# Attention in a fused three-layer kernel: the eight query products, one run of 24 matmuls each, divided into blocks between the scores and the weights

## The reference, cut to what matters

```python
def nsa_mixer(h, w_q, w_o, k_cmp, v_cmp, k_sel, v_sel, k_win, v_win):
    proj = h @ w_q
    q = proj[..., :NSA_HEADS * NSA_HEAD_DIM].reshape(bsz, s_len, NSA_KV_HEADS, NSA_GROUP, NSA_HEAD_DIM)
    q_rot = partial_rope(q, jnp.arange(s_len))
    ...
        s = jnp.einsum("bqhgd,bchd->bhgqc", qc, k_cmp) * scale
        p_cmp = masked_softmax(s, (cmp_end[None, :] <= t[:, None])[None, None, None], axis=-1)
        ...
        o = g[..., 0:1] * o_cmp + g[..., 1:2] * o_sel + g[..., 2:3] * o_win
```

## Time and profile before

| what | value |
|---|---|
| median of three runs | 2632.68 us |
| span of the profiled execution | 2629.4 us |
| TensorE, ScalarE, VectorE, GpSimd busy | 96%, 41%, 46%, 37% |
| mean granted TensorE clock | 0.990 |
| attention steps on TensorE | from 929.7 to about 1161 us |

### The profile page before, as it was taken

One profiled execution on the slowest core, in us unless ns is written; L12 is line 12 of the kernel. 1 busy time (PEld: TensorE's weight loads), 2 busy tenths in 40 slices (PEclk: granted clock), 3 DMA queues, 4 the chain that ended last, 5 costly groups with the idle time before them and its releaser, 6 DMA issues.

```text
span 2629.4 us, 36734 instructions
## 1 busy us (share of the span) xinstructions
PE 2511.7 (96%) x13336; PEld 2048.5 (78%) x13336; DVE 1204.0 (46%) x2013; ACT 1067.6 (41%) x1678; POOL 976.4 (37%) x431
## 2 busy tenths in 40 slices
PE   4999989999999989999999999999899999999998
PEld 2877768888888756669888888788668888988887
DVE  6777776656545657645111127653122112631112
ACT  3466644322224346655222236734442323542232
POOL 1433334555554210024444443302114455353453
PEclk9999999999999999999999999999999999999999
DMA  6533344577653210012333232201113333232331
GB/s 255 182 106 120 105 126 131 190 243 237 216 177 130 93 36 19 19 43 66 100 97 105 89 103 69 76 9 56 42 32 101 105 107 113 64 111 87 98 105 56
DMA packets 75762, 277.33 MB, mean 105 GB/s; under 512 B 8528, under 2 KB 10960, under 8 KB 74224
## 3 DMA queue, kind: packets, MB, share of 16 engines
q1 hardware_dynamic: 56672, 201.66, 24.4%
q10 hardware_dynamic: 18960, 73.87, 8.1%
HBM read 272.54 MB, written 2.16 MB: 104 GB/s over the span
## 4 chain that ended last, share of the span: by engine, by line
PE 84%; DVE 7%; ACT 3%; issue 2%; DMA 2%; ACTq 1%; SPq 0%; DVEq 0%
PE G L293 30%; PE STAT_G L293 30%; PE B L306 2%; PE B L587 2%; PE B L293 2%; PE B L2398 1%; DMA const<-in_const 1%; PE B L1342 1%; PE STAT_G L306 1%; PE G L306 1%; PE NRM L1379 1%; ACTq L1108 1%; PE G L587 1%; PE STAT_G L587 1%; PE B L1671 1%
## 5 line engine op out<-in xcount | busy, mean ns | idle before, releaser
L278 POOL TENSOR_TENSOR w_lo<-raw,w_hi 128x1024 fp32r<-128x1024 f32 x375 | 937.5, 2512 | 1601.8 <-ACT w_hi L270 1585.6
L270 ACT ACTIVATE w_hi<-raw 128x1024 fp32r<-128x1024 f32 x375 | 386.4, 1051 | 308.7 <-PE STAT_G L293 127.3
L293 PE MATMUL G<-h_hi,w_hi 128*128 128x512 f32 x888 | 352.0, 396 | 0.1
L293 PE MATMUL STAT_G<-h_hi,w_hi 128*128 128x512 f32 x872 | 344.9, 396 | 3.0 <-ACT mod_w L1227 1.6
L293 PE MATMUL G<-h_lo,w_hi 128*128 128x512 f32 x888 | 346.7, 390 | 0.0
L293 PE MATMUL G<-h_hi,w_lo 128*128 128x512 f32 x888 | 346.7, 390 | 0.0
L293 PE MATMUL STAT_G<-h_lo,w_hi 128*128 128x512 f32 x872 | 339.9, 390 | 0.0
L293 PE MATMUL STAT_G<-h_hi,w_lo 128*128 128x512 f32 x872 | 339.8, 390 | 0.0
L347 DVE SCALAR_TENSOR_TENSOR mod_w<-mod_w,const 128x1024 f32<-128x1024 f32 x96 | 178.9, 1880 | 51.8 <-DMA mod_w<-in_modw 51.4
L293 PEld LDWEIGHTS G<-h_hi,w_hi 128*128 128x128 f32 x888 | 167.4, 189 | 38.7 <-issue 4.2
L293 PEld LDWEIGHTS G<-h_lo,w_hi 128*128 128x128 f32 x888 | 167.5, 189 | 35.3 <-issue 1.4
(11 more groups left out here) (562 smaller groups left out, 4341.4 us busy)
## 6 DMA issues: line engine op xcount, KB each, us to landing
raw<-in_units SPq DMA_DIRECT2D x375, 512.0 KB, 3.6
mod_w<-in_modw ACTq DMA_DIRECT2D x96, 512.0 KB, 4.9
mod_first<-in_modw ACTq DMA_DIRECT2D x8, 1024.0 KB, 21.1
acsb<-acs ACTq DMA_DIRECT2D x16, 512.0 KB, 3.6
cw<-in_cw ACTq DMA_DIRECT2D x2, 2048.0 KB, 8.9
x<-in_x SPq DMA_DIRECT2D x1, 2048.0 KB, 26.8
out<-x SPq DMA_DIRECT2D x1, 1024.0 KB, 4.8
out<-x SPq DMA_DIRECT2D x2, 512.0 KB, 3.1
```

The lines of the kernel that those rows point to most:

```text
L270: act.activation(w_hi[s][:, :], raw[s][:, :], ACT.Identity).then_inc(hi_done, 1)
L278: pool.tensor_tensor(w_lo[s][:, :], raw[s][:, :], w_hi[s][:, :].bitcast(F32), ALU.subtract).then_inc(lo_done, 1)
L293: ins = pe.matmul(out[0:m, :], a[s][:, k * P:k * P + m], b[:, c], start=(n == 0 and q == 0), stop=(n == len(blocks) - 1 and q == 2))
```

## The change

The products of query units 1 to 7 are no longer whole. Their eight blocks (three matmuls each) stand in the turns of the unit ahead: for t = 1 two blocks each in a = 0 to 3, for the others one block each at a % 9 = 5, 6, 8, 0, 1 and 2 and two at 3. They follow the scores and precede the turning of weights, but at a % 9 = 3 they follow the turning, as the whole product did. The first block waits for the copy of the previous queries out of `G0` (`qx_done`) where the whole product waited for their rotation. VectorE's exception at a % 9 = 4 goes. ScalarE, GpSimd and the loads keep their order.

```diff
+        q_parts = {}
+        for t in range(1, 8):
+            a0 = NS * (t - 1)
+            for a, k, n in (((0, 0, 2), (1, 2, 2), (2, 4, 2), (3, 6, 2)) if t == 1 else
+                            ((a0 - 4, 0, 1), (a0 - 3, 1, 1), (a0 - 1, 2, 1), (a0, 3, 1), (a0 + 1, 4, 1),
+                             (a0 + 2, 5, 1), (a0 + 3, 6, 2))):
+                q_parts[a] = (t, range(k, k + n))
+
+        def q_part(pe, t, blocks):
+
+            s = (uq + t) % SLOTS
+            for k in blocks:
+                if k == 0:
+                    pe.wait_ge(qx_done, t)
+                    pe.wait_ge(lo_done, uq + t + 1)
+                for q, (a, b) in enumerate(((w_hi, h1_hi), (w_hi, h1_lo), (w_lo, h1_hi))):
+                    ins = pe.matmul(G0[:, :], a[s][:, k * P:(k + 1) * P], b[:, k * T:(k + 1) * T],
+                                    start=(k == 0 and q == 0), stop=(k == KC - 1 and q == 2))
+                if k == KC - 1:
+                    ins.then_inc(unit_done, 1)
...
                     scores(pe, a)
+                if a in q_parts and a % NS != 3:
+                    q_part(pe, *q_parts[a])
                 if 2 <= a < NA + 2:
                     turn_weights(pe, a - 2)
-                if a % NS == 3 and a // NS < 7:
-                    q_product(pe, a // NS + 1)
+                if a in q_parts and a % NS == 3:
+                    q_part(pe, *q_parts[a])
...
-                turned = a % NS == 4 and a // NS < 7
-                if turned:
-                    scaled(a - 1)
                 if a < NA:
                     largest(a)
                 if a == 0:
                     turn(0)
-                if 1 <= a < NA + 1 and not turned:
+                if 1 <= a < NA + 1:
                     scaled(a - 1)
```

More of the change, by code:

```diff
@@ L1314, in positions, with q_product @@
                 ins.then_inc(pos_done, 1)
[L1316 to L1323, removed]
+        def q_product(pe):
+            pe.wait_ge(kx_done, 8)
+            pe.wait_ge(gate_a, 1)
+            product(pe, uq, h1_hi, h1_lo, out=G0)
+        q_parts = {}
[16 more added lines that the diff above has]
+                    ins.then_inc(unit_done, 1)
         def scores(pe, a):
@@ L1384, in nsa_tensor @@
         def nsa_tensor(pe):
-            q_product(pe, 0)
+            q_product(pe)
             compressed(pe, 1)
```

## The result

The changed kernel takes **2640.64 us**, the kernel before 2632.24 us (medians of 20 runs each); the ratio is 1.0036 (95% interval 1.0028 to 1.0045). The prediction was 2641.0 with a range of 2624 to 2655, and "no difference over 0.5%" as the likeliest outcome. The total came out as forecast. Its terms did not: two errors, of 2.2 and 2.4 us, cancelled, as the rows show.

The account below looks back on a forecast made before the run. TensorE, busy 96% of the span, was taken to bound the kernel. Units +5.6, first unit -2.4 and clock +5.0 gave +8.2 us on a span of 2629.4; with 3.3 for the median, 2641 us, range 2624 to 2655.

Parts of the forecast that it names:

- The mechanism: At win qt = 0, the turning of weights would wait 2.4 us for ScalarE's copy, where it waited 0.68.
- TensorE ready at 6.13 us: With two blocks left and one new block ahead, TensorE reaches the win qt = 0 turning 6.13 us after sel qt = 0's.
- Turning at 8.53: ScalarE's prep, query copy, DMA issue and copy of turned weights allow the win qt = 0 turning only at 8.53 us.
- The price of a block: A lone block of three matmuls between mask and turning was taken to cost TensorE 0.78 us, between 0.71 and 0.86.
- +0.94: Each unit 0.94 us longer without the clock (0.59 to 1.34); six units +5.6 us (3.5 to 8.0).
- The clock: Half clock after some of six new 2.4 us stalls at win qt = 0: +5.0 us, 2.5 us a fall.
- at the same rate two of the six stalls: Two of six idle times elsewhere preceded half clock, so two of six new attention stalls would: +5.0 us.
- the clock falls in most stalls: Rival: half clock after four or more win qt = 0 stalls, 2.5 us each; all six +18, 2651 us; chance 0.29.
- six single waits elsewhere: TensorE idle times of 1.7 to 2.8 us in the earlier trace; the clock stayed after four, halved after two.
- The first unit: Blocks of t = 1 fill idle 4.00 and 0.90 us: gain 4.9 at most or nothing, middle taken, -2.4 us.
- VectorE's order: At sel qt = 3, later scaling costs nothing, ready at about 6.5 under ScalarE's list; uncovered, up to 1.2 us a unit.
- The first rival: Blocks fill TensorE's attention waits and nothing new waits, ScalarE's list not holding the turning: -15, 2618 us; chance 0.09.

Follow-up runs that it names:

- e6_sp_dma_dve_order: Changed kernel with the four query-row DMAs issued by SyncE instead of ScalarE and VectorE's exception at a % 9 = 4 put back: 2618.67 us, ratio 0.9948.
- e2_dve_order: Changed kernel with only VectorE's exception at a % 9 = 4 put back (weights scaled ahead of the next largest scores): 2641.79 us, ratio 1.0033.
- e8_first_unit: Changed kernel with only the product of t = 1 divided, later products whole, and VectorE's order of the kernel before: 2632.16 us, ratio 0.9995.
- e5_sp_dma: Changed kernel with the four DMAs that swap query rows issued by SyncE instead of ScalarE: 2632.64 us, ratio 0.9999.
- e3_prep_later: Changed kernel with ScalarE's rounding of later weights (prep) moved to win qt = 2; GpSimd's split moved with it: 2635.26 us, ratio 1.0018.
- e4_place: Changed kernel with the blocks of t = 2 to 7 placed anew, four at sel qt = 2 and two at win qt = 0: 2622.31 us, ratio 0.9961.
- e10_refill_again: Changed kernel with the first block of units 2 to 7 computed four times over, nine useless matmuls filling the stall; second run of that kernel: 2635.75 us, ratio 1.0012.

## Why the prediction was right, and where its steps failed

**The mechanism held.** TensorE ready at 6.13 us after the turning of sel qt = 0: 6.10. Turning at 8.53, released by ScalarE's copy: 8.39 (the list is 0.14 shorter, mostly because `qx` starts 0.95 after `prep` did, not 1.06). Idle 2.2: 2.09 to 2.13 in units 1 to 5, and 2.84 in unit 6, which has no block in front. The waits at cmp, sel qt = 0 and win qt = 1 are gone from the units with blocks.

**The price of a block was mis-sized, slightly.** I took 0.78 between 0.71 and 0.86. From the mask to the turning behind it are 0.87 us with a block between (1033.40 to 1034.27 in `e6_sp_dma_dve_order`) and were 0.12 without: 0.75. The part of the undisturbed unit behind the stall says 0.74: it takes 28.82 - 8.35 = 20.47 us where it took 28.25 - 10.11 = 18.14, so 2.33 for five blocks less 1.38 of delays removed. With the shorter list the unit is +0.57 without the clock, not +0.94; six are +3.4, not +5.6. By the 216 ns a matmul of the Trainium skill (TensorE: Matmul & The Clock Gate, "Back-to-back issue gap") a block would take 0.65, an estimate; this case's trace disagrees, with 0.74 to 0.75.

**The clock was mis-sized the other way.** The step "at the same rate two of the six stalls" failed: five of six, in the profile of the changed kernel and again in that of `e2_dve_order`. The price failed too: 1.57 us for the four falls inside units and 1.1 for the one in unit 6, instead of 2.5. Together 7.4 us, not 5.0. The rival *the clock falls in most stalls* had the count right, but by its price five falls come to 3.2 + 5 x 2.5 = 15.7 us. The rates that I took from six single waits elsewhere did not carry over.

**The first unit:** -2.7, forecast -2.4, which was the middle between two cases and not worked out. The 2.7 hold a fall: in `e8_first_unit`, without one, the first unit gains 4.2. **Sum:** 3.4 + 7.4 - 2.7 = 8.1, which is what the attention measured; the forecast was 8.2. The steps were off by -2.2, +2.4 and -0.3, so that the total came out so close is luck.

**VectorE's order** did cost nothing, but with a margin of 0.95 us and not of 2: the scaled weights came 7.44 us after the turning of sel qt = 0, not at 6.5, since I did not see the split that would run beside the scaling; the turning that needs them came at 8.39. Without ScalarE's cover I allowed up to 1.2 us a unit; it was 27.97 - 26.53 = 1.4 (`e5_sp_dma` and `e6_sp_dma_dve_order`).

**The first rival's time was right for another kernel.** "If ScalarE's list did not hold the turning up": 2618 us. `e6_sp_dma_dve_order` takes the hold away and measures 2618.67.

## What to carry to other kernels

When long work is divided to fill short waits, ask first which list on another engine that long work was covering: here four DMA issues (2.64 us) and a rounding on ScalarE came to light, and a different table for the same blocks turned +8 us into -10. Count a stall of the matrix engine twice, for its length and for the clock afterwards, and test the second by filling it with useless matmuls. An edit that measures nothing alone (VectorE's order) may be the one that counts once the wait in front of it is gone, so try it again after each removal.

## What the runs showed of the hardware that was not expected

**GpSimd's split holds VectorE's scaling up until it is nearly over.** The same pair of scalings of 128x384 f32 takes 0.87 us alone. Beside GpSimd's split it took 2.00 us when it started 0.97 us after the split did (changed kernel), 1.99 after 0.98 (`e5_sp_dma`) and 2.44 after 0.52 (`e3_prep_later`): in each case it ended 0.59 to 0.61 us after the split's end. Only the first of the two scalings is long: 1.61 us in the changed kernel, 0.47 for the second. The reduction that ran into the same split (1036.09 to 1037.32) took 1.23 us, as in the earlier trace rows. The Trainium skill (SBUF — State Buffer, "Who interferes with whom") says that `tensor_scalar` can enter a mode in which it needs the ports that it shares with GpSimd, and that of the two the later "fully blocks" until the first is done. The ends agree in the main: a scaling that had merely been slowed would have ended later the later it started. But the first scaling ends 0.20 to 0.22 us after the split, less than the 0.47 that one takes alone, so it is not shown that nothing of it is done before; nor does a run here show by itself that the ports are the cause.

**The clock falls after idle times of 2.1 us, yet not after each.** Half clock came after five of six stalls in two profiles (2.09 to 2.13 us, and 2.84 in unit 6); of idle times of 1.14 to 1.31 us in units 1 to 5 (`e3_prep_later`, `e5_sp_dma`) none was followed by a fall there. The length of one idle time does not decide it: early in unit 7 TensorE waits 0.98 to 0.99 us for VectorE in all fourteen profiles, and in three of them (`e4_place`, `e5_sp_dma`, `e10_refill_again`) half clock came behind it. The second of the two windows of `e10_refill_again`, at 1146, is such a case.
